# Entry of a two-block fp32 kernel on rows of tokens, and a bank of its own for the fourth output strip

## What is computed

```python
def rmsnorm(x, w):
    xf = xf * lax.rsqrt(jnp.mean(xf * xf, axis=-1, keepdims=True) + EPS)
    return xf.astype(x.dtype) * w
...
    u = rmsnorm(x, norm_mix_w[l])
    proj = u @ w_in[l] + b_in[l]
    cb, cc, cx, q, k, v, g_conv, g_attn = jnp.split(proj, IN_SPLITS, axis=-1)
    q = apply_rope(q.reshape(b, s, N_Q_HEADS, HEAD_DIM), cos, sin)
    k = apply_rope(k.reshape(b, s, N_KV_HEADS, HEAD_DIM), cos, sin)
...
    # end of hybrid_mixer, second block
    return heads.transpose(0, 2, 1, 3).reshape(b, s, MIX_WIDTH) @ w_o
```

## Time and profile before

| | us |
|---|---|
| median of 3 runs | 1873.3 |
| range of the runs | 1873.29 to 1873.73 |
| the profiled execution | 1873.89 |
| its span, first to last instruction | 1872.2 |
| PE busy | 1835.6 (98%) |
| VectorE busy | 995.6 (53%) |
| ScalarE busy | 673.8 (36%) |
| mean granted TensorE clock | 0.996 |

### The profile page before, as it was taken

How to read it: one execution, slowest core, us unless ns; L and a number is a source line. 1 busy time by engine, 2 the same in 40 slices (tenths; PEclk the granted TensorE clock), 3 DMA queues, 4 the chain that set the end, 5 groups by cost and what they waited for, 6 DMA issues and landing times.

```text
span 1872.2 us, 20783 instructions
## 1 busy us (share of the span) xinstructions
PE 1835.6 (98%) x8585; PEld 1526.9 (82%) x8585; DVE 995.6 (53%) x1357; ACT 673.8 (36%) x1008; POOL 38.1 (2%) x73
## 2 busy tenths in 40 slices
PE   6899999999999999999999999999999999999998
PEld 5688888887888888878888888788888778888887
DVE  5555554457777766783433334656767453333332
ACT  5344442234322322342222222464666342232222
POOL 0000000000000000000000000011200000000001
PEclk9999999999999999999999999999999999999999
DMA  3222223254677565333333332321121323333323
GB/s 113 78 79 79 79 79 96 85 155 147 199 223 257 190 202 185 110 87 91 93 98 91 101 96 87 88 57 47 45 68 35 86 79 94 101 92 100 99 87 96
DMA packets 321715, 200.02 MB, mean 107 GB/s; under 512 B 6696, under 2 KB 311126, under 8 KB 321622
## 3 DMA queue, kind: packets, MB, share of 16 engines
q1 hardware_dynamic: 320128, 196.17, 34.9%
q0 software_dynamic: 640, 2.10, 0.4%
q10 hardware_dynamic: 854, 0.43, 0.1%
HBM read 196.57 MB, written 2.10 MB: 106 GB/s over the span
## 4 chain that ended last, share of the span: by engine, by line
PE 93%; DVE 3%; ACT 2%; DMA 0%; issue 0%; SPq 0%; POOL 0%; ACTq 0%; DVEq 0%
PE ps L1349 92%; PE ps L1352 2%; DVE t_b L834 1%; DMA x_in<-in_x 0%; ACT w_hi L376 0%; DVE u_lo L824 0%; DVE u_lo L822 0%; ACT L387 0%; ACT u_hi L403 0%; DVE x L849 0%; DVE u_lo L1217 0%; DVE ssum L812 0%; ACT rstd L389 0%; ACT rstd L390 0%; DVE k_lo L1142 0%
## 5 line engine op out<-in xcount | busy, mean ns | idle before, releaser
L1349 PE MATMUL ps<-u_hi,w_hi 128*128 128x512 f32 x1688 | 667.5, 395 | 8.8 <-DVE u_lo L822 3.3
L1349 PE MATMUL ps<-u_hi,w_lo 128*128 128x512 f32 x1688 | 659.4, 391 | 0.0
L1349 PE MATMUL ps<-u_lo,w_hi 128*128 128x512 f32 x1688 | 659.0, 390 | 0.0
L792 DVE TENSOR_TENSOR w_lo<-w_raw,w_hi 128x1024 fp32r<-128x1024 f32 (+2 forms) x307 | 364.5, 1188 | 271.3 <-ACT w_hi L376 270.5
L376 ACT ACTIVATE w_hi<-w_raw 128x1024 fp32r<-128x1024 f32 (+2 forms) x307 | 314.2, 1024 | 235.8 <-DMA w_raw<-in_w_down 80.0
L1349 PEld LDWEIGHTS ps<-u_hi,w_hi 128*128 128x128 f32 x1688 | 318.3, 189 | 82.2 <-issue 10.8
L1349 PEld LDWEIGHTS ps<-u_hi,w_lo 128*128 128x128 f32 x1688 | 318.0, 188 | 67.4
L1349 PEld LDWEIGHTS ps<-u_lo,w_hi 128*128 128x128 f32 x1688 | 318.4, 189 | 66.3 <-issue 2.4
L1349 PE MATMUL ps<-y_hi,w_hi 128*128 128x512 f32 x656 | 256.0, 390 | 0.0
L1349 PE MATMUL ps<-y_hi,w_lo 128*128 128x512 f32 x656 | 255.4, 389 | 0.0
L1349 PE MATMUL ps<-y_lo,w_hi 128*128 128x512 f32 x656 | 255.2, 389 | 0.0
(11 more groups left out here) (266 smaller groups left out, 1416.8 us busy)
## 6 DMA issues: line engine op xcount, KB each, us to landing
mod_raw<-in_w_mod SPq DMA_DIRECT2D x72, 512.0 KB, 4.8
w_raw<-in_w_in SPq DMA_DIRECT2D x71, 512.0 KB, 3.9
w_raw<-in_w_ffn_up SPq DMA_DIRECT2D x44, 512.0 KB, 4.0
w_raw<-in_w_gate SPq DMA_DIRECT2D x44, 512.0 KB, 3.8
w_raw<-in_w_up SPq DMA_DIRECT2D x44, 512.0 KB, 3.8
w_raw<-in_w_down SPq DMA_DIRECT2D x32, 512.0 KB, 3.9
w_raw<-in_w_ffn_down SPq DMA_DIRECT2D x16, 512.0 KB, 4.1
w_raw<-in_w_down SPq DMA_DIRECT2D x16, 384.0 KB, 3.4
```

The costliest lines, as they stand in the source:

```text
L792: e.tensor_tensor(w_lo[u % SLOTS][:, 0:n_k, :], w_raw[u % SLOTS][:, 0:n_k, :], f32(w_hi[u % SLOTS][:, 0:n_k, :]), ALU.subtract).then_inc(l ...
L1349: return e.matmul(out_, lhsT, rhs, start=start, stop=stop, skip_group_check=skip)
```

## The change

1. **Order of work in the entry.** The square sum is taken on rows of tokens (ScalarE, with the sum as a second output), VectorE scales a row block by its root, and PE transposes the scaled rows into half-width banks (`turn_half`, five banks in turn). ScalarE and VectorE cut u_hi and u_lo from them, 256 tokens at a time.
2. **Strips 0 and 1 in halves of 256 tokens**: strip 0 first half, strip 1 first half, strip 0 second half, strip 1 second half.
3. **Keys and values first**: the order of the strips is 4, 5, 0, 1, 2, 3.
4. **The raw x** is transposed and copied in pairs of tiles between the strips (`turn_x`).
5. **Loads.** The identity and the frequencies come first (129 columns), the other constants after three strips; only the vectors that the entry needs are loaded from ScalarE's queue, the others and the sinks from SP's behind the fourth strip.
6. **Angles and sines**: the angles come on VectorE after the fourth weight cut, the sines on ScalarE behind the third strip's evacuation, and the rotary sums one strip later.
7. **Fourth output strip** in bank 6 (`LATE_BANK`), free once the last step's first head is cut; its weight cuts stand before the last head.

```diff
+LATE_BANK = ATT_BANKS[(N_STEPS - 1) % 2][1]
...
+QKV = (4, 5, 0, 1, 2, 3)
...
-            return ps[:, 3 if u == U["w_o"] + 2 else u % 2, :]
+            return ps[:, {U["w_o"] + 2: 3, U["w_o"] + 3: LATE_BANK}.get(u, u % 2), :]
...
+            e.dma_start(consts[:, 0:N_FIRST], d["consts"][:, 0:N_FIRST]).then_inc(first_in, 16)
+            load_x(0)
+            load_x(1)
+            load_x(2)
+            load_strip(0)
+            load_strip(1)
+            load_x(3)
+            load_strip(2)
+            e.dma_start(consts[:, C_ROT:N_CONST], d["consts"][:, C_ROT:N_CONST]).then_inc(const_in, 16)
+            load_strip(3)
+            for t in range(1, len(VEC_TILES)):
+                load_vec(e, t)
+            e.dma_start(sink_c[:, :], d["sinks"].broadcast_to([P, N_SWA_HEADS])).then_inc(row_landed, 16)
+            e.dma_start(bf_c[:, :], d["b_f_2"].broadcast_to([P, N_FOX])).then_inc(row_landed, 16)
+            for u in range(SLOTS, N_UNITS):
+                e.wait_ge(unit_done, u - SLOTS + 1)
+                load_strip(u)
...
+            def row_norm(tb):
+                if tb == 0:
+                    e.wait_ge(pool_set, 2)
+                e.wait_ge(x_landed[tb], 16)
+                after_own(e.activation(x_norm[:, tb, :], x_in[:, tb, :], ACT.Square, accum_out=ssq[:, tb:tb + 1]))
+                after_own(e.activation(row_r[:, tb:tb + 1], ssq[:, tb:tb + 1], ACT.Ln, bias=EPS_COL[EPS1], scale=1.0 / D_MODEL))
+                e.activation(row_r[:, tb:tb + 1], row_r[:, tb:tb + 1], ACT.Exp, scale=-0.5).then_inc(row_root, 1)
+
+            def first_hi(h, c):
+                if (h, c) == (0, 0):
+                    e.wait_ge(vec_set, 1)
+                e.wait_ge(half_turned, h * KC + c + 1)
+                e.activation(u_hi[:, c, half(h)], half_bank(h, c), ACT.Copy, scale=GAIN["mix"](c)).then_inc(half_hi if h == 0 else u_hi_set, 1)
+
+            e.preload_act_table_set(LN_EXP)
+            for tb in range(3):
+                row_norm(tb)
+            cut_hi(0)
             for c in range(KC):
-                e.wait_ge(x_turned, c + 1)
-                e.activation(x[:, c, :], bank(2 + c % 4), ACT.Copy).then_inc(x_set, 1)
-            squares("mix", lambda c: e.wait_ge(x_set, c + 1))
+                first_hi(0, c)
+            cut_hi(1)
+            row_norm(3)
+            for c in range(KC):
+                first_hi(1, c)
+            cut_hi(2)
+            cut_hi(3)
...
+                if n < 4:
+
+                    for v in (2 * n, 2 * n + 1):
+                        e.wait_ge(x_turned, v + 1)
+                        e.activation(x[:, v, :], bank(2 + v % 2), ACT.Copy).then_inc(x_set, 1)
+                if n == 2:
+                    e.wait_ge(v_turned, 1)
+                    e.activation(v1[:, :, :], bank(6).rearrange("p (t n) -> p t n", n=P), ACT.Copy).then_inc(v_set, 1)
+                    for m in range(2):
+                        e.wait_ge(angle_set, m + 1)
+                        table = (sin_t, cos_t)[m]
+                        e.activation(table, table, ACT.Sin).then_inc(tables_set, 1)
...
                     fox_cut(i, 1)
+                    cut_hi(u + 3)
                     e.wait_ge(at_valued, 2 * i + 2)
...
+            for tb in range(3):
+                scale_row(tb)
+            e.wait_ge(vec_set, 1)
+            cut_lo(0)
+            for c in range(KC):
+                first_lo(0, c)
+            cut_lo(1)
+            scale_row(3)
+            for c in range(KC):
+                first_lo(1, c)
+            cut_lo(2)
+            for t in range(1, len(VEC_TILES)):
+                rows = VEC_ROWS[t]
+                e.wait_ge(vec_turned, len(VEC_TILES))
+                e.tensor_copy(vec[:, t * P:t * P + rows], ps[:, 7, t * P:t * P + rows]).then_inc(vec_set, 1)
+            cut_lo(3)
...
+            for n in range(6):
+                cut_lo(U["qkv"] + n + 2)
+                if n >= 2:
+                    rope(n - 2)
+            rope(4)
...
+                if u == U["w_o"] + OPEN_STRIPS:
+
+                    e.wait_ge(p_cut, cuts_before(N_STEPS - 1) + 3)
+                elif u >= 2:
...
+            e.wait_ge(warm_set, 1)
+            keep_busy(30, 0)
+            e.wait_ge(first_in, 16)
+            e.wait_ge(vec_landed[0], 16 * len(VEC_TILES[0]))
+            turn(ps[:, 7, 0:VEC_ROWS[0]], vec_rows[0:VEC_ROWS[0], 0, :], VEC_ROWS[0]).then_inc(vec_turned, 1)
+            keep_busy(10, 0)
+            for tb in range(2):
+                e.wait_ge(row_scaled, tb + 1)
+                for c in range(TURN_BANKS):
+                    turn_half(tb, c)
+                keep_busy((8, 14)[tb], 0)
+            for k in range(KC):
+                half_strip(0, 0, k)
+                if TURN_BANKS + k < KC:
+                    turn_half(0, TURN_BANKS + k)
+                    turn_half(1, TURN_BANKS + k)
+            for k in range(KC):
+                half_strip(1, 0, k)
+                if k in (1, 5):
+                    tb = 2 + k // 5
+                    e.wait_ge(row_scaled, tb + 1)
+                    for c in range(TURN_BANKS):
+                        turn_half(tb, c)
+            for k in range(KC):
+                half_strip(0, 1, k)
+                if TURN_BANKS + k < KC:
+                    turn_half(2, TURN_BANKS + k)
+                    turn_half(3, TURN_BANKS + k)
+            for t in range(1, len(VEC_TILES)):
+                e.wait_ge(vec_landed[t], 16 * len(VEC_TILES[t]))
+                e.wait_ge(vec_set, 1)
+                rows = VEC_ROWS[t]
+                turn(ps[:, 7, t * P:t * P + rows], vec_rows[0:rows, t, :], rows).then_inc(vec_turned, 1)
+            for k in range(KC):
+                half_strip(1, 1, k)
...
+            rotate(0)
+            turn_x(0)
+            unit(U["qkv"] + 2, u_act)
+            u = U["qkv"] + 1
             e.wait_ge(bank_read[u % 2], u // 2 + 1)
-            e.wait_ge(vec_set, 3)
             for tb in range(TB):
                 ins = turn(ps[:, 6, tb * P:(tb + 1) * P], v_t[:, tb * P:(tb + 1) * P])
             ins.then_inc(v_turned, 1)
-            e.wait_ge(roped, 5)
+            turn_x(1)
+            unit(U["qkv"] + 3, u_act)
+            rotate(1)
+            turn_x(2)
+            unit(U["qkv"] + 4, u_act)
+            rotate(2)
+            turn_x(3)
+            unit(U["qkv"] + 5, u_act)
+            rotate(3)
+            e.wait_ge(roped, 1)
+            e.wait_ge(x_set, KC)
             for kv in range(2):
                 mm(bank(2 + kv), consts[:, C_DUP + kv * P:C_DUP + (kv + 1) * P], k1[:, 0, :], True, True).then_inc(k_copied, 1)
+            rotate(4)
```

More of the change, by code:

```diff
@@ L217, in two_blocks @@
             gate = sb("gate", [P, 3 * TB * N_FOX], F32, r1)
+        with ExitStack() as r1:
+            x_norm = sb("x_norm", [P, TB, D_MODEL], F32, r1)
         with ExitStack() as r1:
@@ L335, in two_blocks, with half, half_bank, load_vec @@
         EPS_OF = {"mix": EPS1, "ffn0": EPS1, "ffn1": EPS1 * EPS2, "mix2": EPS2, "ffn2": EPS2}
+        ssq, row_r = small[:, 32:36], small[:, 36:40]
+        def half(h):
+            return slice(h * HALF, (h + 1) * HALF)
+        def half_bank(h, c):
+            return ps[:, 2 + (h * KC + c) % TURN_BANKS, 0:HALF]
         def factor(s, c):
             return gains[:, (3 + s) * KC + c:(3 + s) * KC + c + 1]
+        def load_vec(e, t):
+            for name, n in VEC_TILES[t]:
+                r = VEC[name] - t * P
+                src = d[name]
+                axes = "abcd"[:len(src.shape)]
+                flat = src.rearrange(" ".join(axes) + " -> (" + " ".join(axes) + ")") if len(axes) > 1 else src
+                e.dma_start(vec_rows[r:r + n, t, :], flat.rearrange("(r p) -> r p", p=P)).then_inc(vec_landed[t], 16)
@@ L376, in cut_hi @@
                 e.activation(w_hi[u % SLOTS][:, 0:n_k, :], w_raw[u % SLOTS][:, 0:n_k, :], ACT.Copy).then_inc(hi_cut, 1)
-            def squares(which, ready):
-                n0 = SQ[which] * KC
-                for c in range(KC):
-                    ready(c)
-                    if n0 + c >= 2:
-                        e.wait_ge(summed, n0 + c - 1)
-                    e.activation(t_b[c % 2][:, :], x[:, c, :], ACT.Square).then_inc(squared, 1)
             def root(which):
@@ L424, in scalar @@
[L424 to L430 removed]
+            load_vec(e, 0)
@@ L815, in norm @@
                 f = FILL[which]
-                order = [FILL[n] for n in ("mix", "ffn0", "ffn1", "mix2", "ffn2")].index(f)
+                order = [FILL[n] for n in ("ffn0", "ffn1", "mix2", "ffn2")].index(f)
                 n0 = order * KC
@@ L1425, in tensor, with turn_half @@
[L1425 to L1431 removed]
+            def turn_half(tb, c):
+                n = tb // 2 * KC + c
+                if n >= TURN_BANKS:
+                    v = n - TURN_BANKS + 1
+                    if v <= KC:
+                        e.wait_ge(half_lo, v)
+                    else:
+                        e.wait_ge(u_lo_set, v - KC)
```

(23 more changed lines are left out.)

167 lines of the change are left out of this document (63 added, 104 removed).

## The result

The changed kernel takes 1847.11 us (median of 4 runs, 1846.91 to 1847.39) against 1873.34 (1873.29 to 1873.73): ratio 0.9862, 95% interval 0.9847 to 0.9877. The forecast was 1847.4, in a range of 1843 to 1855. The profiled execution's span is 1845.6 us where it was 1872.2, 26.6 less; the sum had 25.9.

A forecast was written before the change was run, and what follows sets the result against it. PE was taken to bound the kernel, holding 93% of the chain that ended last, so only its idle or low-clock time could be won. Entry 21.8 plus output strips 4.1 gave 25.9 us, hence 1847.4; range 1843 to 1855.

The forecast's parts named there:

- Fourth output strip: Output strips: the fourth starts at 1462.9 instead of 1466.07, the fifth at 1469.1 instead of 1473.2; gain 4.1 us.
- Loads and rows: Entry: first row block lands near 5.4, three blocks done near 10.4, strip 0 lands at 12.0 and decides.
- First product: Entry: PE's first product of strip 0 at 14.8 us instead of 32.90.
- products on constants: Entry, before the first product: early dummy products on PE, said to lie in time when PE has nothing.
- Halves: Entry, strips 0 and 1: half-width cuts on VectorE set the pace at 0.45 us each; the halves end at 29.5.
- Silu and keys: Entry: silu waits for VectorE's small vectors, keys' evacuation ends at 30.4, PE idles 0.9 us.
- Rotations and strips: Entry from the keys on: rotation 0.9, pair of x tiles 0.9, then strip; convolution starts at about 62.0.
- Low keys' cover: Convolution: VectorE's last low keys ready at about 65, PE asks at 67.5, a cover of 2 us.
- no wait of PE appeared in the convolution: Rival, convolution: PE waits for VectorE 1 to 2 us at up to four window heads, 1851 to 1855; chance 0.06.
- the outputs won: Rival, output strips: the fifth waits as long as the fourth did, nothing won there, 1851.5; chance 0.06.
- the first rival: Entry halves: low clock makes 96 products cost 0.21 instead of 0.12, 9.3 us, 1.5 hidden, about 1855.2; chance 0.11.
- The range's upper end: Whole kernel, 1855: late strip 1.2, halves 1.7, rotations 2.6, outputs 0.6, and most of two rivals.

The follow-up runs named there:

- the positions late: Changed kernel with the load of the positions taken off ScalarE's queue and issued by SyncE behind the fourth strip of weights: 1846.41 us.
- both experiments: Changed kernel without the fourth output strip's own bank and early cuts, 1851.31 us; kernel before with these alone, 1869.57 us.
- the next profile of the changed kernel: Changed kernel run again with nothing altered, beside two later kernels on one chip: 1848.58 us.
- the strips whole: Changed kernel with strips 0 and 1 in products of 512 columns, started when both blocks of rows are cut: 1853.91 us.

## Why the prediction was right, point by point

- **Loads and rows.** First row block at 6.19 (forecast 5.4), third at 9.90 (8.9), pitch of a block on ScalarE 1.62 (1.65), strip 0 cut from 11.71 (12.0). The forecast let the strip decide, with the rows done 1.6 us before it (10.4 and 12.0). In fact both came at once: ScalarE was done with the third block at 11.61, 1.2 late, and the strip landed at about 2.74 + 8.9 = 11.6, 0.4 early. So this time was hit with its margin gone, and with the positions late ScalarE's rows decided, not the strip. In ten further profiles of this entry the first block came at 5.1 to 5.65 in eight, and at 6.36 and 6.64 in two.
- **First product** 14.64 (14.8). The products on constants were said to lie in time when PE has nothing. That was true by a hair, as PE waited 0.17 us behind them; in the profile with the positions late it waited for nothing, and they were the bound.
- **Halves.** VectorE's pace 3.62 us for eight, 0.45 each, as taken. TensorE starts strip 1 at 19.38 (19.1, a wait for its low half being in the forecast), and the four halves end at 18.4, 23.5, 27.1 and 30.20 (18.3, 23.0, 26.5, 29.5): each a little longer than costed, and the end 0.7 late. Of 0.3, the late start of strip 1, the cause is known: its high half stood on ScalarE behind the last pieces of the first rows, at 17.02, which the forecast had not looked at. The 96 half-width products were given as 11.2 us; at the forecast's own 0.12 each they are 11.5.
- **Silu and keys.** 0.9 us of wait were forecast and none came. The table load at 27.93 doesn't wait for the silu's input; it runs beside VectorE's copies (28.14 to 28.59), the silu follows at 29.23 and the keys' evacuation ends before PE asks at 30.20. So the rotation starts at 30.20 where 30.4 was said. The kernel before had shown such a load: that of its sines ran at 41.17, the first sine, whose input was late, at 46.06. The Trainium skill (ScalarE: Activation LUTs, What ACT_TABLE_LOAD costs) would have 1.4 us more here; the rows after again have the silu right behind the load (27.93 + 1.28, then 29.23), so the row was the right guide.
- **Rotations and strips.** Rotation, pair of x tiles and strip 0.9 + 0.9 + 5.44 = 7.2; 44.22 to 51.42 is 7.20. Sines at 47.16 without a table load (47.6), convolution at 61.66 (62.0). Entry gain 22.1 (21.8).
- **Low keys' cover.** 2 us were forecast; k_lo ends at 66.49 and PE's scores start at 67.51, so 1.0 was left, which was enough.
- **Fourth output strip.** The fifth strip's first product stands 1446.59 - 1440.65 = 5.9 us behind the fourth's (6.2), the load not yet there when ScalarE asks (0.77 us). Gain 4.5 (4.1), 4.3 in both experiments; the low clock of 1.7 was counted in.
- **Rivals.** None came: no wait of PE appeared in the convolution, and the outputs won. That the halves didn't run at the low level is told by their products, 0.12 us apart from 14.84 on. The granted clock reads 1.00 from 14 to 30 us, but by this the prediction couldn't have been proved wrong, since it reads 1.00 without the products on constants too, where the products come at the low level's pace. Without the products on constants the first rival comes true for 5 us and costs 1.35 us, not 8: it had no bound on how long the low clock holds, though the strip behind the output wait showed it ending within one.
- **Where it was lucky.** The halves' 0.7 too little and the silu's 0.9 too much nearly cancel. The two parts came out 0.3 and 0.4 better than forecast, which makes the sum's 0.7, and the entry moves by itself: the same entry ended 0.4 us earlier in the next profile of the changed kernel, and the rest came 1.5 us later. A forecast within 0.3 us of the median is closer than that allows. The range's upper end has no full working either: the terms named for it add to 6.1 us, 1853.5, where 1855 was taken.

## What to carry to other kernels

A wait of TensorE of some 3 us costs its own length and then, mostly, a low clock. Behind one and the same wait of 3.1 us, products ran at the low level for 3.4 us in one kernel and for 5.7 in another, at half of that in cost; behind a wait of 2.5 us they did in one profile and not in another. So price such a gap at one and a half to twice its length, and expect the price to change from one execution or kernel to the next. Look in the queue of the engine that waits for a late input, not at that input: the two sines cost 8 us in the kernel before (5.3 of waiting and 2.8 of low clock), ahead of an evacuation that needed neither. Split a step in halves when its inputs come in halves, but then give the other halves of its operands their place in the same queue, or the wait only moves.

## What the runs showed of the hardware

- **VectorE's copies stop while GpSimd fills memory.** Three copies of 128x128 take 1.0 us each beside 0.95 us memsets, 0.18 to 0.23 with the memsets held back, and in two profiles they got through only when all four memsets were over, at 5.0 us. The Trainium skill (SBUF — State Buffer, Who interferes with whom) has it so: copies and casts can need the pair of ports that VectorE shares with GpSimd, whoever is first holds it for a whole instruction, and the other is blocked. The runs agree on the blocking, and add that the loser can lose four times in a row. Who was first can't be read from the starts: the first cast starts at 1.04, the first large memset at 1.11, and the cast still ends behind it.
- **The granted clock reads 1.00 at the start while TensorE runs at the low level.** Without the products on constants it reads 1.00 for 14 to 20 us (window below), where 256-column products start 0.21 us apart until 19.6. Only the distance between the products tells there.

```profile
16.00:18.00 2.00, 2.00 (x11) 1.00 1.09 337
```

- **When the clock rises varies.** The same 30 products on constants took 6.23, 5.17, 6.32 and 5.42 us in four profiles with the same start, at 3.23; at 0.21 us each they are 6.3. Between two of these profiles, which had TensorE busy up to it, the first product moved by 0.9 us (14.40 and 13.53).
- **A table load runs ahead of its activation's input** (27.93, with the vectors there only at 28.59); with the strips whole it was over 4.13 us ahead of its silu.
